# Attention scores as two TensorE passes instead of three, with the key's two parts stacked over 128 partitions

## What is computed

```
proj = xn @ w_in                       # q, k and v of both mixers
sc = einsum('bnqhgd,bnkhd->bnhgqk', qc, kb) * (dh ** -0.5) + bias
p = softmax(sc)                        # mixer A: with a sink logit
o = einsum('bnhgqk,bnkhd->bnqhgd', p, vb)
merged = gates_a * (att_a @ w_branch_a) + gates_b * (att_b @ w_branch_b)
h = h + merged @ w_out ;  h = h + square(relu(hn @ w_mlp_in)) @ w_mlp_out
```

## Time and profile before

| | us |
|---|---|
| median of 3 runs (2528.43 to 2529.54) | 2528.63 |
| the profiled execution, its own time | 2527.88 |
| its span in the trace | 2526.1 |
| TensorE busy | 2501.1 (99%) |
| DVE busy | 1671.6 (66%) |
| ACT busy | 980.0 (39%) |

### The profile page before, as it was taken

The page is one execution under the profiler, slowest core; times in us unless marked ns, Lnnn a source line. Parts: engine busy times, 40 slices in busy tenths (PEclk is TensorE's granted clock), DMA queues, the critical chain, the costliest instruction groups (busy, mean ns, idle before and its releaser), DMA issues.

```text
span 2526.1 us, 34808 instructions
## 1 busy us (share of the span) xinstructions
PE 2501.1 (99%) x14354; PEld 2205.9 (87%) x14354; DVE 1671.6 (66%) x2284; ACT 980.0 (39%) x1247; POOL 184.1 (7%) x169
## 2 busy tenths in 40 slices
PE   9999999999999999999999999999999999999998
PEld 8898888888888888888899999999998888888886
DVE  5566555555333333523698888888889888877897
ACT  4444543345222222312344333333334444444445
POOL 0000000000001101001000000000011011110010
PEclk9999999999999999999999999999999999999999
DMA  7776777787789999852234443333448666566652
GB/s 257 206 212 188 196 199 204 194 215 204 217 237 265 246 246 257 244 196 89 78 109 138 130 134 131 129 131 128 131 157 330 231 225 205 205 234 229 229 192 109
DMA packets 192225, 483.54 MB, mean 191 GB/s; under 512 B 13104, under 2 KB 117696, under 8 KB 182224
## 3 DMA queue, kind: packets, MB, share of 16 engines
q1 hardware_dynamic: 180672, 347.26, 41.0%
q0 software_dynamic: 11264, 134.23, 21.1%
q10 hardware_dynamic: 144, 0.02, 0.0%
HBM read 460.44 MB, written 155.23 MB: 244 GB/s over the span
## 4 chain that ended last, share of the span: by engine, by line
PE 95%; DVE 2%; DMA 1%; issue 0%; POOL 0%; ACT 0%; SPq 0%; DVEq 0%; POOLq 0%; ACTq 0%
PE bank L1516 31%; PE bank L1518 30%; PE bank L1517 30%; PE bank L1622 1%; PE bank L1605 1%; DMA landing<-in_w_out 1%; POOL raw_forms L1426 0%; DMA landing<-in_w_in 0%; DVE up_lo L1239 0%; DVE form_lo_b L1208 0%; DMA raw_forms<-hidden_rows 0%; DVE at_lo L1095 0%; PE bank L1523 0%; DVE w_lo L901 0%; ACT up_hi L784 0%
## 5 line engine op out<-in xcount | busy, mean ns | idle before, releaser
L901 DVE TENSOR_TENSOR w_lo<-landing,w_hi 128x1024 fp32r<-128x1024 f32 x200 | 248.8, 1244 | 467.8 <-ACT w_hi L595 467.6
L595 ACT ACTIVATE w_hi<-landing 128x1024 fp32r<-128x1024 f32 x200 | 212.1, 1060 | 667.9 <-PE bank L1518 656.5
L784 ACT ACTIVATE up_hi<-up_raw 128x1792 fp32r<-128x1792 f32 x128 | 218.0, 1704 | 413.5 <-PE bank L1518 388.6
L1516 PE MATMUL bank<-xn_hi,w_hi 128*128 128x512 f32 x928 | 367.1, 396 | 2.3 <-DVE w_lo L901 1.7
L1518 PE MATMUL bank<-xn_hi,w_lo 128*128 128x512 f32 x928 | 361.8, 390 | 0.0
L1517 PE MATMUL bank<-xn_lo,w_hi 128*128 128x512 f32 x928 | 361.5, 390 | 0.0
L831 ACT ACTIVATE ring<-down_raw 128x1024 fp32r<-128x1024 f32 x224 | 237.5, 1061 | 310.7 <-PE bank L1518 310.7
L1323 DVE TENSOR_TENSOR ring<-down_raw,ring 128x1024 fp32r<-128x1024 f32 x224 | 285.5, 1284 | 68.5 <-ACT ring L831 68.4
L1239 DVE TENSOR_TENSOR up_lo<-up_raw,up_hi 128x1792 fp32r<-128x1792 f32 x128 | 261.9, 2046 | 75.4 <-ACT up_hi L784 75.4
L1516 PE MATMUL bank<-form_hi_b,up_hi 128*128 128x256 f32 x896 | 254.7, 284 | 3.4 <-DVE up_lo L1239 3.4
L1516 PE MATMUL bank<-form_hi_a,up_hi 128*128 128x256 f32 x896 | 254.7, 284 | 3.2 <-DVE up_lo L1239 3.2
(11 more groups left out here) (174 smaller groups left out, 4857.1 us busy)
## 6 DMA issues: line engine op xcount, KB each, us to landing
down_totals<-in_down_blocks POOLq DMA_DIRECT2D x64, 1024.0 KB, 9.4
up_raw<-in_up_units SPq DMA_DIRECT2D x128, 512.0 KB, 3.5
down_raw<-down_totals SPq DMA_DIRECT2D x128, 512.0 KB, 4.4
down_raw<-in_down_blocks SPq DMA_DIRECT2D x96, 512.0 KB, 4.3
landing<-in_w_in SPq DMA_DIRECT2D x72, 512.0 KB, 5.6
landing<-in_w_gate SPq DMA_DIRECT2D x64, 512.0 KB, 5.4
landing<-in_w_out SPq DMA_DIRECT2D x32, 512.0 KB, 3.7
hidden_rows<-hidden_out SPq DMA_DIRECT2D x32, 512.0 KB, 3.3
```

Source lines behind the costliest of these rows:

```text
L595: nc.scalar.activation(w_hi[:, u % SPLIT, :], landing[:, u % LAND, :], ACT.Copy).then_inc(unit_hi, 1)
L784: nc.scalar.activation(up_hi[n % 2], up_raw[n % 3][:, 1:8, :], ACT.Copy).then_inc(up_hi_done, 1)
L901: nc.vector.tensor_tensor(w_lo[:, s, :], landing[:, u % LAND, :], w_hi[:, s, :].bitcast(F32), ALU.subtract).then_inc(unit_lo, 1)
L1516: nc.tensor.matmul(dst, a_hi, b_hi, start=start, stop=False, **kw)
```

## The change

The key's hi and lo part no longer lie in two tensors of their own. In `k_parts` each half of a key block (64 partitions, one head) has its hi part in its own 64 partitions and its lo part in the other 64. The query's hi part of one head is copied twice, into partitions 0 to 63 and 64 to 127 of `q_twice_early` (or, for the last four heads, of a free part of `q_hi`). One matmul over all 128 rows then gives hi·hi + hi·lo; a second one, over 64 rows, adds lo·hi. ACT makes the two copies (`double_q`, 64x512 each) in the slot before the scores, and PE waits for a new semaphore, `q_doubled`. A key block's hi and lo parts are now made in two instructions of 64 partitions each, on ACT and on DVE, instead of one of 128. `q_twice_early` lies in the last two blocks of `stream`, which are written by the last four heads only.

```diff
+            def double_q(h):
+                mixer, g = ("a", h // 4) if h < A_HEADS else ("b", (h - A_HEADS) // 4)
+                act.wait_ge(proj_hi, ready_count(block_no("q", mixer, g)))
+                if h >= 2:
+                    act.wait_ge(scores_done, h - 1)
+                if h == HEADS - 4:
+                    act.wait_ge(scores_done, HEADS - 4)
+                r, qb = q_place(h)
+                nc.scalar.activation(q_twice(h)[0:DH], q_hi[r:r + DH, qb, :].bitcast(F32), ACT.Copy)
+                nc.scalar.activation(q_twice(h)[DH:P], q_hi[r:r + DH, qb, :].bitcast(F32), ACT.Copy).then_inc(q_doubled, 1)
...
             def stage(n):
...
                 if n % KU == 0:
                     evacuate(n // KU - 1)
+                if n + 1 in SCORES_AT:
+                    double_q(SCORES_AT.index(n + 1))
...
+                if kind == "k":      # evacuate, ACT
+                    nc.scalar.activation(k_half((mixer, i), 0, 0), scaled[0:DH, 0:2, :], ACT.Copy)
+                    nc.scalar.activation(k_half((mixer, i), 0, 1), scaled[DH:P, 0:2, :], ACT.Copy).then_inc(proj_hi, 1)
+                    return
...
+                if kind == "k":      # block_lo, DVE
+                    for half in range(2):
+                        r = half * DH
+                        ins = nc.vector.tensor_tensor(k_half((mixer, i), 1, half), scaled[r:r + DH, 0:2, :],
+                                                      k_half((mixer, i), 0, half).bitcast(F32), ALU.subtract)
...
-                s = slot_of(mixer, g)
+                keys = k_parts[:, slot_of(mixer, g), kb, r // DH, :]
+                pe.wait_ge(q_doubled, h + 1)
                 for t, (first, n, bk, col, _) in enumerate(head_tiles(h)):
                     qs, ks = slice(t * P, (t + 1) * P), slice(first * P, first * P + n)
-                    ins = product(bank[:, bk, col:col + n], q_hi[r:r + DH, qb, qs], q_lo[r:r + DH, qb, qs],
-                                  k_hi[r:r + DH, s, kb, ks], k_lo[r:r + DH, s, kb, ks], True, True)
+                    dst = bank[:, bk, col:col + n]
+                    nc.tensor.matmul(dst, q_twice(h)[:, qs], keys[:, ks], start=True, stop=False)
+                    ins = nc.tensor.matmul(dst, q_lo[r:r + DH, qb, qs], keys[r:r + DH, ks], start=False, stop=True)
```

More of the change, by code:

```diff
@@ L154, in build @@
         bank = ctx.enter_context(nc.psum_tensor("bank", [P, 8, 512], F32))
+        spare_features = ExitStack()
+        sb("spare_pad", [P, 14 * SEQ], F32, spare_features)
+        q_twice_early = sb("q_twice_early", [P, 2, SEQ], F32R, spare_features)
+        spare_features.close()
         stream = sb("stream", [P, TT * D])
@@ L183, in build @@
         q_lo = sb("q_lo", [P, 4, SEQ], F32R, first_phase)
-        k_hi = sb("k_hi", [P, 2, 2, SEQ], F32R, first_phase)
-        k_lo = sb("k_lo", [P, 2, 2, SEQ], F32R, first_phase)
+        k_parts = sb("k_parts", [P, 2, 2, 2, SEQ], F32R, first_phase)
         v_parts = sb("v_parts", [P, 2, TT, 4, 2 * DH], F32R, first_phase)
@@ L284, in v_part, with k_half, q_twice, q_place @@
             return v_parts[:, s, :, :, part * DH:(part + 1) * DH].rearrange("p t h d -> p (t h) d")
+        def k_half(i, part, half):
+            r = (part + half) % 2 * DH
+            return k_parts[r:r + DH, slot_of(*i), :, half, :]
+        def q_twice(h):
+            return q_hi[:, h % 2, :] if h >= HEADS - 4 else q_twice_early[:, h % 2, :]
+        def q_place(h):
+            if h < A_HEADS:
+                return h // 4 % 2 * DH, h % 4
+            g, hh = (h - A_HEADS) // 4, h % 4
+            return hh % 2 * DH, 2 * (g % 2) + hh // 2
         def block_parts(c):
@@ L295, in block_parts @@
             s = slot_of(mixer, i)
-            if kind == "k":
-                return scaled[:, 0:2, :], k_hi[:, s], k_lo[:, s]
             return (scaled[:, 0:2, :].rearrange("p b (t h d) -> p (b t h) d", t=2, h=4),
@@ L329, in build @@
         proj_hi = sem("proj_hi")
+        q_doubled = sem("q_doubled")
         proj_ready = sem("proj_ready")
@@ L974, in block_lo @@
                 dve.wait_ge(proj_hi, ready_count(c))
+                kind, mixer, i = BLOCKS[c]
+                if kind == "k":
[3 more added lines that the diff above has]
+                                                      k_half((mixer, i), 0, half).bitcast(F32), ALU.subtract)
+                    ins.then_inc(proj_ready, 1)
+                    return
                 src, hi, lo = block_parts(c)
@@ L1587, in scores @@
                                            for kind in "qk"))
[L1588 to L1591, removed]
-                s = slot_of(mixer, g)
+                r, qb = q_place(h)
+                kb = g // 2 if mixer == "a" else hh // 2
+                keys = k_parts[:, slot_of(mixer, g), kb, r // DH, :]
+                pe.wait_ge(q_doubled, h + 1)
                 for t, (first, n, bk, col, _) in enumerate(head_tiles(h)):
                     qs, ks = slice(t * P, (t + 1) * P), slice(first * P, first * P + n)
-                    ins = product(bank[:, bk, col:col + n], q_hi[r:r + DH, qb, qs], q_lo[r:r + DH, qb, qs],
-                                  k_hi[r:r + DH, s, kb, ks], k_lo[r:r + DH, s, kb, ks], True, True)
+                    dst = bank[:, bk, col:col + n]
+                    nc.tensor.matmul(dst, q_twice(h)[:, qs], keys[:, ks], start=True, stop=False)
+                    ins = nc.tensor.matmul(dst, q_lo[r:r + DH, qb, qs], keys[r:r + DH, ks], start=False, stop=True)
                 ins.then_inc(scores_done, 1)
```

## The result

| | us |
|---|---|
| before, median | 2528.84 |
| changed kernel, median of 4 runs (2547.37 to 2552.03) | 2549.79 |
| ratio, with its 95% interval | 1.008 (1.0068 to 1.0093) |
| the profiled execution, its own time and span | 2549.34 and 2547.5 |

A forecast was written before the change was run, and what follows sets the result against it. TensorE, busy for 99% of the span, was taken as the bound. One pass fewer -17.8, changes of rows +35.0, first key block +2.1 gave 19.3 us more, 2548 us; range 2538 to 2555.

The forecast's parts named there:

- The bound: TensorE is busy for 99% of the span, so a microsecond saved or added in the scores counts in full.
- The changes of rows: Scores: each switch between 128-row and 64-row matmuls costs 0.15 to 0.20 us; 35.0 us more over 32 heads.
- the pass: Scores: one pass goes from each of a head's four tiles; 17.8 us less over all heads.
- The key block at the start: After the first block, two key instructions instead of one on ACT and DVE delay PE; 2.1 us more.
- The copies: ACT's doubling of the query before the scores, 0.60 us a copy, 38 us in all, fits ACT's idle time; costs nothing.
- The first: Scores: changes of rows inside a head cost nothing; 15.7 us faster, 2513 us; chance 0.09.
- the second: Scores: only one direction of row change costs, 17.3 us, cancelling the saving; 2530 us; chance 0.05.
- The third: Scores: PE waits 1 us for ACT's copies in some eight slots; 8 us on top, 2556 us; chance 0.04.
- the slots that the prediction named: Some eight ACT slots before scores where an evacuation stands ahead of the doubling, the only ones where copies could come late.

The follow-up runs named there:

- 64-row version: The changed kernel with its first pass cut to 64 rows, leaving out the product with the key's low part; 2516.10 us, ratio 0.9951.
- moved key block: The changed kernel with the first key block's hi and lo parts made behind the split of weight unit 8; 2546.70 us, ratio 1.007.
- 128-row version: The changed kernel with the query's low part doubled too, all passes over 128 rows, first key block's parts behind unit 8's split; 2502.95 us, ratio 0.9898.

## Why the prediction came out

**The bound.** Right. PE is busy for 99% of the span as before, and what its timeline loses in the scores and at the start (21.3 us) the span loses too (21.4).

**The changes of rows.** Right, in mechanism, count and size. The steps of the changed kernel are the undisturbed ones plus 0.15 (0.26 against 0.11), 0.19 (0.31 against 0.12) and 0.20 (0.43 against 0.23). Behind 384 columns, which the forecast had to guess, it is 0.19 (0.37 against 0.18). Head 9 takes 0.64 us more (forecast 1.10 - 0.47 = 0.63) and head 16, which follows a unit, 0.43 (forecast 1.09 - 0.64 = 0.45 on the mean). Over all heads it is 17.6 us, where the forecast had 17.2. Each half of that sum is measured as well, by the 64-row version: the pass is worth 17.8 us (forecast 17.8) and the changes of rows 35.4 (forecast 35.0), so the agreement isn't two errors that cancel. The three orders of the same eight matmuls then give 8, 4 and 2 changes of rows in a head and 2549.8, 2527.4 and 2516.8 us.

**The key block at the start.** The mechanism was right and the size short: 2.4 us in place of 2.1 on the chain, and 1.3 us more for the stretch at half clock behind it, which the prediction didn't have. The 2.1 came from steps of 0.96 and 1.14 us between records of 1.06 and 1.23 us, which overlap a little; in the changed kernel the records don't overlap, and the second key instruction adds 1.09 us on ACT (DVE starts at 54.49 instead of 53.40) and 1.35 on DVE (`w_lo` follows after 2.49 instead of 1.14). Together the start costs 3.7 us against 2.1, and this 1.6 with the 0.4 of the scores is the difference between the 21.3 us of the trace and the 19.3 of the forecast.

**The copies.** Right: no wait in the trace, and measured alone no time beyond the 2.8 us that the interval leaves. A copy takes 0.63 us, not 0.60.

**The rivals.** The first (the seams of before belong to the border of the routine) and the second (only one direction costs) both fall by the timeline of the changed kernel, where either direction inside the routine has the same length. The third (copies too late) falls for this kernel, but its mechanism is real: with two copies more in a head, five heads wait, four of them in the slots that the prediction named, those with an evacuation ahead of the copies.

## What to carry to other kernels

In these traces (fp32r, 128 to 512 columns) a matmul over 64 rows next to one over 128 costs 0.15 to 0.20 us more than one next to its like, on either side, as much as a whole pass of 128 to 512 columns (0.11 to 0.23 us). No run has 64-row matmuls on different halves of the partitions next to one another, so whether that counts as a change too stays open. So when contraction dimensions are mixed, count the changes of rows in PE's queue before counting matmuls, and either put equal rows together (here 33 us from the order alone) or fill the rows with a copy so that there is no change at all (here 44 us against the changed kernel with the moved key block, and 26 us against the kernel before). And what a change puts ahead of the first use of a resource at the start, where nothing covers it, counts in full, even if the same instruction is free everywhere else.

## What the runs showed of the chip that was not expected

Two things. An idle stretch of PE of 2.7 us, 2.4 longer than the one that was there before, was followed in four traces of five by a granted clock of 0.50 and products 0.43 us apart, so that the stall cost half as much again as its own length; in the fifth the clock stayed at 1.00, as it does at this place in every trace without the hole. What decides between the two is not shown. And filling the rows gains more than the pass removed: the version whose products all use 128 rows runs as many matmuls as the changed kernel, does the most arithmetic of all, and is the fastest, since the 64-row scores had paid for a change on the way in and one on the way out in every head all along. By the steps of the kernel before that is 0.34 to 0.40 us a head, 12 us over 32 heads; between the traces of the 64-row and the 128-row version it is 59.0 - (51.1 - 2.5 of waits) = 10.4 us. The 17.8 of the pass and these 10.4, less the 2.5 of waits, make the 25.5 us by which the span of the 128-row version (2500.6) lies below that of the kernel before (2526.1).
